# One transfer of 1 MB per unit of streamed weights in place of two transfers of 512 KB

## The chip, the cores and the metric

One core of one Trainium2 chip (trn2) runs the kernel. The metric is the device time of one execution in microseconds (us); lower is better.

## What is computed

One layer of a streaming encoder for 640 tokens (512 of a prompt, 8 x 16 of running streams), all in float32, width 2048. Cut to what matters:

```
p  = x @ w_in                                     # 8448 columns: q, k, v of two mixers, two gates
yA = chunk_band_attention(...); yB = sliding_window_attention(...)
h  = LayerNorm(alpha*x + (sigmoid(gA)*(yA@w_proj_a) + sigmoid(gB)*(yB@w_proj_b)) @ w_out)
y  = LayerNorm(alpha*h + PEER(h))                 # 128*128 experts of one neuron, 8 heads, 16 picks per head

PEER: q = h @ w_query; scores against two sets of 128 keys; top 16 of the 16*16 sums of two top 16s
      act = gelu(u_table[picks] . h); out = sum(gate * act * v_table[picks])
```

## The kernel before

All matrix products go through one stream of weights. `wstream` is a list of units; a unit is 128 partitions x 2048 float32 values, 1 MB, 8 KB in each partition. The program walks through 484 units (`SEGMENTS`, `TOTAL`): 34 of the q, k, v projection for the first 256 tokens, 32 of the gates, 16 each of projection, output and query, the same once more for the other 384 tokens, and then 256 units of the expert tables u and v for the 320 tokens that are computed densely. Each unit is 16 k steps.

A float32 product is made of three products of the reduced type fp32r: the weights are split into a high part (a copy into the reduced type) and a low part (what is left), and so are the moving operands. `k_step`, `act_step` and `part` issue the three matmuls of a k step (high x high, high x low, low x high), so a unit is 48 matmuls. Per unit `n`, with slot `s = n % 2`:

- SP loads the unit into `raw[s]` (`w_raw`), in two halves of 1024 values per partition, `HALVES` (`load`, lines 448 to 451). Each half has a semaphore of its own, `raw_half[s][h]`, and waits until POOL has subtracted the same half of unit `n - 2`: `low_first` counts the first halves, `split_done` the second ones.
- ACT copies each half into `w_hi[s]` (`split_high`, line 969). It waits for the half's landing and for PE to have read the same half of unit `n - 2` (`half_read`, `unit_done`). `split_high(n + 2, 0)` stands in ACT's program ahead of the evacuation of unit `n`, `split_high(n + 2, 1)` behind it.
- POOL subtracts: `w_lo = w_raw - w_hi`, a half at a time (`low`, line 507), when ACT's copy is done.
- PE starts a unit at `low_first` and goes on with its second half at `split_done`.

Every engine takes its instructions in the order of its program. So there are two slots in `w_raw` and two in `w_hi` and `w_lo`, and a half of `w_raw` is free again when POOL has subtracted it.

Beside this stream, 320 tokens get their experts by gathers: `ITEMS` is a list of 649 steps, of which 640 are an indirect DMA of 128 rows of 8 KB (1 MB) from the u or the v table into one of four buffers (`rows`, `fetch`, line 525) and a pass of DVE over them (lines 1483 and 1486). `deal` spreads the steps over the units from `GATHER_AT` on, by the rates in `RATES`, two per unit for most of the last 192. POOL issues the gather of step `r + 4` right behind a `low` of the unit to which step `r` was dealt, after DVE has released its buffer (`rows_used`). DVE takes the steps in order too, between its other work for the units.

The last 192 units are, first, eight groups of 8 u units (activations, line 851) and 8 v units (output, line 906), for which ACT loads 1280 KB of `gate_matrix` each (`load_gates`), and then 64 v units in eight groups whose activations were computed early and are loaded again with the gates (`load_early`: one load of 1280 KB and eight of 160 KB per group).

```
act.wait_ge(raw_half[s][h], 16 * (n // 2) + 16)
if n >= 2:
    act.wait_ge((half_read, unit_done)[h], n - 1)
act.activation(w_hi[s][:, HALVES[h]], raw[s][:, HALVES[h]], ACT.Copy).then_inc(hi_late, 1)
```

Of the kernel before, what the change touches and what calls it, by code (L numbers as in the profile page):

```python
# [54 lines left out]
HALVES = (slice(0, D // 2), slice(D // 2, D))  # L55
# [10 lines left out]
AT = {}  # L66
# [175 lines left out]
def build(nc, x_t, wstream, u_rows, v_rows, cka, cva, ckb, cvb, rext, negs, bp_b, bs_b, sinks, lnp, lnrow, subk, consts, pt_out, y_out, n_out):  # L242
# [3 lines left out]
    ds = bass.ds  # L246

    with ExitStack() as ctx:
# [3 lines left out]
        def sb(name, shape, dt=f32):  # L252
            return ctx.enter_context(nc.sbuf_tensor(name, shape, dt))

        def sem(name):
            return ctx.enter_context(nc.semaphore(name))
# [8 lines left out]
        raw = [sb(f"w_raw{s}", [P, D]) for s in range(2)]  # L265
# [126 lines left out]
            return ap[..., FROM[ph]:FROM[ph] + WIDTH[ph]]  # L392


        raw_half = [[sem(f"raw_half{s}_{h}") for h in range(2)] for s in range(2)]
        hi_late, low_first, split_done, half_read, unit_done = (
            sem(n) for n in ("hi_late", "low_first", "split_done", "half_read", "unit_done"))

# [46 lines left out]

        @block.sync
        def _(sp):
            def load(n, unit, s, h):
                sp.wait_ge((low_first, split_done)[h], n - 1)
                sp.dma_start(raw[s][:, HALVES[h]], wstream[:, ds(unit, 1), HALVES[h]].rearrange("p a c -> p (a c)")) \  # L450
                    .then_inc(raw_half[s][h], 16)

            for s in range(2):
                if s:
                    sp.wait_ge(mv_in[1], 16)
                for h in range(2):
                    sp.dma_start(raw[s][:, HALVES[h]], wstream[:, s, HALVES[h]]).then_inc(raw_half[s][h], 16)

            def table(dst, src):
                sp.dma_start(dst, src).then_inc(tab_done, 16)  # L460

            def bias_table(n):

                rt, n_r = rext.tensor, rext.shape[1]
                if n == 0:
                    table(bp_a[:, 64:P, :], bass.AP(rt, 63, [[n_r, 16], [-1, 64], [1, 512]]))
                elif n == 1:
                    table(bp_a[:, 0:64, 0:448], bass.AP(rt, 127, [[n_r, 16], [-1, 64], [1, 448]]))
                elif n < 6:
                    h = slice(4 * n - 8, 4 * n - 4)  # L470
                    table(bp_a[h, 0:64, 448:512], negs[h])
                elif n < TABLES:
                    b = DEC_T * (n - 6)
                    table(bs_a[:, b:b + DEC_T, :], bass.AP(rt, 383, [[n_r, 16], [-1, 16], [1, 144]]))

            for name, unit, count in SEGMENTS:
                if name == "qkv":
                    for i in range(1, count // 2):
                        for s in range(2):
                            for h in range(2):  # L480
                                load(2 * i + (AT[name] + s), 2 * i + (unit + s), s, h)
                            bias_table(2 * i - 2 + s)
                    continue
                first = 0
                if count == 2:
                    for s in range(2):
                        for h in range(2):
                            load(AT[name] + s, unit + s, s, h)
                    continue
                with sp.Fori(first, count // 2) as i:  # L490
                    for s in range(2):
                        for h in range(2):
                            load(2 * i + (AT[name] + s), 2 * i + (unit + s), s, h)

            for k in range(KT_N):
                sp.wait_ge(ln_out, k + 1)
                sp.dma_start(y_out[k], r_acc[:, k, :]).then_inc(y_out_done, 16)
            sp.wait_ge(y_out_done, 16 * KT_N)
# [458 lines left out]
        def _(act):  # L957
# [3 lines left out]
            def split_high(n, h):  # L961

                s = n % 2
                if n >= TOTAL:
                    return
                act.wait_ge(raw_half[s][h], 16 * (n // 2) + 16)
                if n >= 2:
                    act.wait_ge((half_read, unit_done)[h], n - 1)
                act.activation(w_hi[s][:, HALVES[h]], raw[s][:, HALVES[h]], ACT.Copy).then_inc(hi_late, 1)  # L969
# [4 lines left out]
            def load(dst, src, into):  # L974
                act.dma_start(dst, src).then_inc(into, 16)
# [6 lines left out]
            def qkv_slot(n, i, ph, between=None):  # L982

                s, w = n % 2, WIDTH[ph]
                split_high(n + 2, 0)
                if between is not None:
                    between()
                act.wait_ge(unit_done, n + 1)
                free_ev(s)
                act.activation(ev[s][:, 0:w], acc(s, ph), ACT.Copy, scale=SCALE if i >= ROW_QA else 1.0).then_inc(qkv_evac, 1)  # L990
                split_high(n + 2, 1)
                act.wait_ge(qkv_evac, 2 + N_QKV * ph + i + 1)
                load(cut(pt_out[i], ph), ev[s][:, 0:w], qkv_stored[s])
                stores["qkv"][s] += 1
# [23 lines left out]
            for k in range(KT_N):  # L1018
                if k % 4 == 0:
                    act.wait_ge(mv_in[k // 4], 16)  # L1020
                copy_high(0, k, Rw[0][:, k, :])
                if k % 4 == 3:
                    split_high(k // 8, k // 4 % 2)
# [257 lines left out]
            n = AT["b2"]  # L1281
# [17 lines left out]
            for i in range(B_CHUNKS[4]):  # L1299
                n = AT["b4"] + i  # L1300
# [33 lines left out]
            for m in range(TAIL):  # L1334
                n = AT_EARLY + m
# [11 lines left out]
                if m in (1, 3):  # L1347
                    h = m // 2
# [653 lines left out]
```

## Time and profile before

| | us |
|---|---|
| median of 3 runs | 4365.65 |
| lowest, highest | 4357.78, 4372.58 |
| the profiled execution | 4363.35 |
| its span, first to last instruction | 4361.4 |

The difference of 2 us between the profiled execution and its span lies before the first and behind the last instruction. "Busy" of an engine is the time in which one of its instructions ran; for PE the ends are modelled, and matmuls overlap, so the mean of one is about twice the distance between two. The DMA share is the mean busy share of the core's 16 DMA engines; where packets overlap it can pass 1. In the queues, `q0` holds the DMAs that POOL issues (gathers among them), `q1` those of SP and `q10` those of ACT. PEclk is the granted clock of TensorE as a share of its full 2.4 GHz.

### The profile page before, as it was taken

To read this page: it belongs to the slowest core of one execution; us is meant where nothing else is said; L and a number is where in the kernel's file an instruction comes from. 1 tells how busy PE (TensorE), PEld (TensorE's weight loads), DVE (VectorE), ACT (ScalarE), POOL (GpSimd) and SP (SyncE) were. 2 spreads that over 40 slices of the span, in tenths; PEclk is the share of its full clock that TensorE was granted. 3 is DMA by queue.
4 is the path that set the end of the run, shared out by engine and by line. 5 is a ranking of instruction groups with operands and counts; after the bars stand their busy time and mean duration, and the time that the engine had idled before them with its cause. 6 is when DMAs were issued, how large, how long until landed. Compare 5 with 4: busy or idle time off the path is not lost. (4 is left out here: it accounts for less than half of the span.)

```text
span 4361.4 us, 71495 instructions
## 1 busy us (share of the span) xinstructions
PE 4062.1 (93%) x26789; PEld 3894.4 (89%) x26789; DVE 2803.3 (64%) x4041; ACT 1666.8 (38%) x2837; POOL 2980.6 (68%) x1624
## 2 busy tenths in 40 slices
PE   8999999999999999889799799999999997988997
PEld 8988889999977777889799799999999997988886
DVE  3122222278466688798697677576776766789885
ACT  4433444442233344332333266633333332322333
POOL 7843457675754455678357767688888987888884
PEclk9988999999999999899899899999999999999998
DMA  8755446554998899899246999999999999999993
GB/s 293 225 161 158 132 135 207 163 169 140 375 367 343 335 372 364 336 386 412 93 129 210 389 330 344 332 391 413 417 418 412 413 413 386 412 414 398 414 400 101
DMA packets 366152, 1341.34 MB, mean 308 GB/s; under 512 B 35969, under 2 KB 148481, under 8 KB 280449
## 3 DMA queue, kind: packets, MB, share of 16 engines
q0 software_dynamic: 93760, 682.66, 38.1%
q1 hardware_dynamic: 146992, 515.57, 34.3%
q10 hardware_dynamic: 125200, 140.62, 9.2%
q8 instruction: 105, 1.72, 0.2%
q14 instruction: 95, 0.77, 0.0%
HBM read 1277.73 MB, written 65.80 MB: 308 GB/s over the span
## 5 line engine op out<-in xcount | busy, mean ns | idle before, releaser
L507 POOL TENSOR_TENSOR w_lo<-w_raw,w_hi 128x1024 fp32r<-128x1024 f32 x968 | 2342.3, 2421 | 1129.3 <-ACT w_hi L969 1112.8
L969 ACT ACTIVATE w_hi<-w_raw 128x1024 fp32r<-128x1024 f32 x968 | 1022.1, 1057 | 1469.9 <-DMA w_raw<-in_wstream 869.8
L1486 DVE SCALAR_TENSOR_TENSOR banks<-rows,act_n,banks 128x2048 f32<-128x2048 f32 x320 | 752.6, 2352 | 224.7 <-DMA rows<-in_v_rows,idx_all 221.8
L1483 DVE CUSTOM_DVE_ANT_0 rows<-rows,banks 128x2048 f32<-128x2048 f32 x320 | 728.7, 2282 | 260.7 <-DMA rows<-in_u_rows,idx_all 259.8
L906 PE MATMUL banks<-weighted,w_hi 128*128 128x320 f32 x3072 | 694.3, 315 | 59.4 <-DVE weighted L1853 28.9
L572 PE MATMUL banks<-mv,w_hi 128*128 128x256 f32 x3648 | 693.4, 292 | 18.6 <-POOL w_lo L507 12.7
L572 PE MATMUL banks<-mv_hi,w_hi 128*128 128x384 f32 x1824 | 638.1, 350 | 56.1 <-ACTq L1223 21.5
L851 PE MATMUL banks<-mv_hi,w_hi 128*128 128x320 f32 x2048 | 647.5, 316 | 39.9 <-POOL w_lo L507 36.6
L851 PE MATMUL banks<-mv_lo,w_hi 128*128 128x320 f32 x2048 | 635.6, 310 | 0.0
L851 PE MATMUL banks<-mv_hi,w_lo 128*128 128x320 f32 x2048 | 635.4, 310 | 0.0
L572 PE MATMUL banks<-mv_lo,w_hi 128*128 128x384 f32 x1824 | 620.7, 340 | 0.0
L572 PE MATMUL banks<-mv_hi,w_lo 128*128 128x384 f32 x1824 | 620.2, 340 | 0.0
L572 PEld LDWEIGHTS banks<-mv,w_hi 128*128 128x128 f32 x3648 | 589.0, 199 | 29.3 <-issue 13.4
L906 PEld LDWEIGHTS banks<-weighted,w_hi 128*128 128x128 f32 x3072 | 523.8, 192 | 69.7 <-DVE work L1878 33.1
L572 PE MATMUL banks<-mv,w_lo 128*128 128x256 f32 x1824 | 527.5, 289 | 0.0
L906 PE MATMUL banks<-weighted,w_lo 128*128 128x320 f32 x1536 | 481.2, 313 | 0.0
L572 PEld LDWEIGHTS banks<-mv_hi,w_hi 128*128 128x128 f32 x1824 | 350.7, 192 | 105.8 <-issue 81.4
L851 PEld LDWEIGHTS banks<-mv_hi,w_hi 128*128 128x128 f32 x2048 | 387.6, 189 | 49.7 <-POOL w_lo L507 40.2
L525 POOL DMA_INDIRECT rows<-in_u_rows,idx_all x320 | 321.2, 1004 | 117.9 <-issue 53.3
L851 PEld LDWEIGHTS banks<-mv_lo,w_hi 128*128 128x128 f32 x2048 | 387.8, 189 | 0.0
L851 PEld LDWEIGHTS banks<-mv_hi,w_lo 128*128 128x128 f32 x2048 | 386.9, 189 | 0.0
L525 POOL DMA_INDIRECT rows<-in_v_rows,idx_all x320 | 310.3, 970 | 93.1 <-issue 46.8
(180 smaller groups left out, 5412.1 us busy)
## 6 DMA issues: line engine op xcount, KB each, us to landing
w_raw<-in_wstream SPq DMA_DIRECT2D x968, 512.0 KB, 7.0
gate_matrix<-work ACTq DMA_DIRECT2D x20, 1024.0 KB, 13.9
work<-gate_matrix ACTq DMA_DIRECT2D x16, 1280.0 KB, 10.9
early_act<-work ACTq DMA_DIRECT2D x64, 160.0 KB, 6.3
out_p<-work ACTq DMA_DIRECT2D x34, 192.0 KB, 3.6
gate_scratch<-work ACTq DMA_DIRECT2D x32, 192.0 KB, 7.8
work<-gate_scratch ACTq DMA_DIRECT2D x16, 384.0 KB, 10.2
rows<-in_lnrow POOLq DMA_DIRECT2D x6, 1024.0 KB, 9.3
```

The lines of the kernel that those rows point to most:

```text
L507: pool.tensor_tensor(w_lo[s][:, part], raw[s][:, part], w_hi[s][:, part].bitcast(f32), ALU.subtract) \
L525: pool.indirect_dma_start(rows, None, u_rows if kind == "u" else v_rows, bass.IndirectOffsetOnAxis(ap=idx_at[blk][:, pick:pick + 1], axis= ...
L572: ins = pe.matmul(out, a[s][:, P * k:P * k + P], b[ph][:, k, :], start=(k == first and n == 0), stop=(k == last and n == 2))
L851: last = pe.matmul(banks[:, bank, 0:ND], a[s][:, P * k:P * k + P], b[1][:, k, G3:], start=(k == 0 and n == 0), stop=(k == KT_N - 1 and n = ...
L906: last = pe.matmul(banks[:, dt % 4, 0:ND], a[s][:, at:at + P], b[z][:, e, :], start=(e == 0 and n == 0), stop=(e == EG - 1 and n == 2))
L969: act.activation(w_hi[s][:, HALVES[h]], raw[s][:, HALVES[h]], ACT.Copy).then_inc(hi_late, 1)
L1483: ins = dve.tensor_tensor_reduce(rows, rows, nat, 1.0, 0.0, ALU.mult, ALU.add, weight)
L1486: ins = dve.scalar_tensor_tensor(nat, rows, weight, nat, ALU.mult, ALU.add)
```

## The change

Each unit is loaded by one transfer of 128 x 2048 values, 8 KB per partition, with one semaphore per slot, `raw_in[s]`. SP issues it when both halves of unit `n - 2` are subtracted (`split_done`). Both of ACT's copies wait for this one semaphore. Copies, subtractions and matmuls are made in halves as before.

```diff
--- before.py
+++ after.py
@@ -392,7 +392,7 @@
             return ap[..., FROM[ph]:FROM[ph] + WIDTH[ph]]
 
 
-        raw_half = [[sem(f"raw_half{s}_{h}") for h in range(2)] for s in range(2)]
+        raw_in = [sem(f"raw_in{s}") for s in range(2)]
         hi_late, low_first, split_done, half_read, unit_done = (
             sem(n) for n in ("hi_late", "low_first", "split_done", "half_read", "unit_done"))
 
@@ -445,16 +445,14 @@
 
         @block.sync
         def _(sp):
-            def load(n, unit, s, h):
-                sp.wait_ge((low_first, split_done)[h], n - 1)
-                sp.dma_start(raw[s][:, HALVES[h]], wstream[:, ds(unit, 1), HALVES[h]].rearrange("p a c -> p (a c)")) \
-                    .then_inc(raw_half[s][h], 16)
+            def load(n, unit, s):
+                sp.wait_ge(split_done, n - 1)
+                sp.dma_start(raw[s][:, :], wstream[:, ds(unit, 1), :].rearrange("p a c -> p (a c)")).then_inc(raw_in[s], 16)
 
             for s in range(2):
                 if s:
                     sp.wait_ge(mv_in[1], 16)
-                for h in range(2):
-                    sp.dma_start(raw[s][:, HALVES[h]], wstream[:, s, HALVES[h]]).then_inc(raw_half[s][h], 16)
+                sp.dma_start(raw[s][:, :], wstream[:, s, :]).then_inc(raw_in[s], 16)
 
             def table(dst, src):
                 sp.dma_start(dst, src).then_inc(tab_done, 16)
@@ -477,20 +475,17 @@
                 if name == "qkv":
                     for i in range(1, count // 2):
                         for s in range(2):
-                            for h in range(2):
-                                load(2 * i + (AT[name] + s), 2 * i + (unit + s), s, h)
+                            load(2 * i + (AT[name] + s), 2 * i + (unit + s), s)
                             bias_table(2 * i - 2 + s)
                     continue
                 first = 0
                 if count == 2:
                     for s in range(2):
-                        for h in range(2):
-                            load(AT[name] + s, unit + s, s, h)
+                        load(AT[name] + s, unit + s, s)
                     continue
                 with sp.Fori(first, count // 2) as i:
                     for s in range(2):
-                        for h in range(2):
-                            load(2 * i + (AT[name] + s), 2 * i + (unit + s), s, h)
+                        load(2 * i + (AT[name] + s), 2 * i + (unit + s), s)
 
             for k in range(KT_N):
                 sp.wait_ge(ln_out, k + 1)
@@ -963,7 +958,7 @@
                 s = n % 2
                 if n >= TOTAL:
                     return
-                act.wait_ge(raw_half[s][h], 16 * (n // 2) + 16)
+                act.wait_ge(raw_in[s], 16 * (n // 2) + 16)
                 if n >= 2:
                     act.wait_ge((half_read, unit_done)[h], n - 1)
                 act.activation(w_hi[s][:, HALVES[h]], raw[s][:, HALVES[h]], ACT.Copy).then_inc(hi_late, 1)
```

On SP, the loop over the last units, before:

```order
L490 ISA
L450 ISA [waits low_first]
L450 DMA w_raw<-in_wstream 128x1024
L450 ISA [waits split_done]
L450 DMA w_raw<-in_wstream 128x1024
L449 REGISTER_ALU
L450 ISA [waits low_first]
L450 DMA w_raw<-in_wstream 128x1024
L450 ISA [waits split_done]
L450 DMA w_raw<-in_wstream 128x1024
L490 REGISTER_ALU
```

and now:

```order
L486 ISA
L450 ISA [waits split_done]
L450 DMA w_raw<-in_wstream 128x2048
L449 REGISTER_ALU
L450 ISA [waits split_done]
L450 DMA w_raw<-in_wstream 128x2048
L486 REGISTER_ALU
```

Four issues for two units have become two, each behind the second half's subtraction.

On ACT, at the end of a group of v units and the first u unit of the next (`work<-gate_matrix` is the gates' load, `banks<-banks` the activation of a u unit), before:

```order
L969 ACTIVATE w_hi<-w_raw 128x1024 [waits unit_done,raw_half0_1]
L975 DMA work<-gate_matrix 128x2560 [waits w_prod]
L969 ACTIVATE w_hi<-w_raw 128x1024 [waits half_read,raw_half1_0]
L969 ACTIVATE w_hi<-w_raw 128x1024 [waits unit_done,raw_half1_1]
L969 ACTIVATE w_hi<-w_raw 128x1024 [waits half_read,raw_half0_0]
L969 ACTIVATE w_hi<-w_raw 128x1024 [waits unit_done,raw_half0_1]
```

and now:

```order
L964 ACTIVATE w_hi<-w_raw 128x1024 [waits unit_done,raw_in0]
L970 DMA work<-gate_matrix 128x2560 [waits w_prod]
L964 ACTIVATE w_hi<-w_raw 128x1024 [waits half_read,raw_in1]
L964 ACTIVATE w_hi<-w_raw 128x1024 [waits unit_done,raw_in1]
L964 ACTIVATE w_hi<-w_raw 128x1024 [waits half_read,raw_in0]
L964 ACTIVATE w_hi<-w_raw 128x1024 [waits unit_done,raw_in0]
```

No instruction of ACT has moved. Both copies of a slot now wait for the same semaphore. On PE, DVE and POOL nothing has moved.

## Rows read from the trace of the kernel before

**Rows 1.** The page: busy time and share of each engine.

```profile
PE 4062.1 (93%) x26789; PEld 3894.4 (89%) x26789; DVE 2803.3 (64%) x4041; ACT 1666.8 (38%) x2837; POOL 2980.6 (68%) x1624
```

**Rows 2.** Windows: us, busy (x instructions) per engine, PEclk, DMA share, GB/s.

```profile
593.00:826.00 233.00, 228.90 (x1793) 225.43 (x1791) 52.04 (x124) 102.89 (x141) 173.64 (x72) 0.99 0.64 192
...
2821.00:3309.00 488.00, 466.58 (x3084) 458.14 (x3083) 337.54 (x330) 164.66 (x204) 424.71 (x247) 0.98 1.01 407
3309.00:3807.00 498.00, 462.17 (x3074) 459.15 (x3073) 349.90 (x295) 161.29 (x201) 421.65 (x249) 0.97 1.01 407
3807.00:4254.00 447.00, 404.64 (x2644) 391.89 (x2642) 394.25 (x360) 141.40 (x169) 366.05 (x213) 0.99 1.01 406
```

**Rows 3.** Windows: eight u units, and the border to the v units behind them.

```profile
3549.15:3605.85 56.70, 56.66 (x384) 56.07 (x383) 41.07 (x30) 20.29 (x29) 52.95 (x32) 1.00 1.02 418
3605.85:3618.80 12.95, 8.92 (x50) 8.92 (x51) 8.97 (x9) 4.43 (x7) 10.73 (x7) 0.87 1.02 418
```

**Rows 4.** Waits, 2821 to 4254 us: waiting, released by: us, times, longest.

```profile
ACT w_hi L969 <- DMA w_raw<-in_wstream: 773.7, 308, 6.5
DVE banks L1486 <- DMA rows<-in_v_rows,idx_all: 155.5, 127, 4.3
POOL w_lo L507 <- ACT w_hi L969: 133.5, 179, 8.4
DVE rows L1483 <- DMA rows<-in_u_rows,idx_all: 131.9, 97, 6.7
...
PE banks L906 <- DVE work L1878: 29.9, 29, 3.0
PE banks L906 <- DVE weighted L1853: 28.9, 11, 4.9
PE banks L906 <- POOL w_lo L507: 17.9, 11, 4.6
PE banks L851 <- POOL w_lo L507: 16.3, 4, 14.2
```

**Rows 5.** The chain that ended last, 3840 to 3870 us: start, us, what.

```profile
3851.81 13.16 DMA w_raw<-in_wstream
3864.97 0.02 issue
3864.99 1.07 ACT w_hi L969
3866.06 0.07 issue
3866.13 2.42 POOL w_lo L507
```

**Rows 6.** DMA, 2821 to 4254 us: queues; issues with median us to landing.

```profile
q0 software_dynamic: 49060, 357.23, 60.7%
q1 hardware_dynamic: 52613, 191.54, 33.8%
...
w_raw<-in_wstream SPq DMA_DIRECT2D x365, 512.0 KB, 10.9
work<-gate_matrix ACTq DMA_DIRECT2D x16, 1280.0 KB, 10.9
work<-early_act ACTq DMA_DIRECT2D x32, 160.0 KB, 20.1
x_raw<-early_act ACTq DMA_DIRECT2D x32, 160.0 KB, 28.1
```

**Rows 7.** Timeline of SP and POOL from 3599 us.

```profile
3601.89 0.33 SPq L450 DMA_DIRECT2D w_raw<-in_wstream  x1
...
3599.32 2.41 POOL L507 TENSOR_TENSOR w_lo<-w_raw,w_hi 128x1024 fp32r<-128x1024 f32 x1 [0.25 <-ACT w_hi L969]
3601.88 0.95 POOL L525 DMA_INDIRECT rows<-in_v_rows,idx_all  x1
3603.09 2.41 POOL L507 TENSOR_TENSOR w_lo<-w_raw,w_hi 128x1024 fp32r<-128x1024 f32 x1 [0.26 <-ACT w_hi L969]
```

**Rows 8.** DMA issues: half loads from 700 to 1000 us; a 1 MB store.

```profile
w_raw<-in_wstream SPq DMA_DIRECT2D x87, 512.0 KB, 3.5
...
block_h<-work ACTq DMA_DIRECT2D x1, 1024.0 KB, 3.9
```

**Rows 9.** Timeline of ACT and POOL in the light stretch.

```profile
788.69 1.06 ACT L969 ACTIVATE w_hi<-w_raw 128x1024 fp32r<-128x1024 f32 x1 [1.82 <-PE banks L572]
791.57 1.06 ACT L969 ACTIVATE w_hi<-w_raw 128x1024 fp32r<-128x1024 f32 x1 [1.82 <-PE banks L572]
...
789.83 2.40 POOL L507 TENSOR_TENSOR w_lo<-w_raw,w_hi 128x1024 fp32r<-128x1024 f32 x1 [0.48 <-ACT w_hi L969]
```

**Rows 10.** Timeline of ACT at the start, the copies of unit 1.

```profile
12.95 1.06 ACT L969 ACTIVATE w_hi<-w_raw 128x1024 fp32r<-128x1024 f32 x1 [0.77 <-DMA w_raw<-in_wstream]
...
15.14 1.04 ACT L969 ACTIVATE w_hi<-w_raw 128x1024 fp32r<-128x1024 f32 x1
```

## The prediction

> **What bounds the kernel now.** The page's summary comes first [rows 1]: PE is busy for 93% of the span, the other engines for 38 to 68%. PE is therefore the engine to watch, and a change in the loads can give back only what PE loses while it waits. The table of windows says where that is [rows 2]. From 2821 to 4254 us the DMA engines are busy for a share of 1.01 in all three windows, at 406 to 407 GB/s. One unit is 48 matmuls (16 k steps of three), so 3084, 3074 and 2644 matmuls are 64.3, 64.0 and 55.1 units, and a unit takes 7.60, 7.78 and 8.11 us. Eight units that run without a stall take 56.70 us for 384 matmuls, 7.09 each, with the granted clock at 1.00 [rows 3]; right behind them 12.95 us hold 50 matmuls, a stall of nearly 6 us at the border from u units to v units, while DMA stays at 1.02 and 418 GB/s. These 1433 us lose about 0.7 us per unit, and DMA is full throughout. In the light stretch from 593 to 826 us DMA is busy for 0.64 [rows 2].
>
> The waits of that stretch say who is late [rows 4]: ACT waits 773.7 us for `w_raw`, POOL 133.5 us for ACT, DVE 155.5 + 131.9 us for gathered rows. Seen from PE, 17.9 + 16.3 us go to POOL's `w_lo` and 29.9 + 28.9 us to DVE. The chain shows the loop in one piece [rows 5]: transfer 13.16, copy 1.07, subtraction 2.42, about 0.2 between them, then the next transfer into the same half: 16.9 us for two units, 8.45 each. So a half buffer goes round as fast as its transfer lands, and the transfer is slow since DMA is shared. The queues show how [rows 6]: 365 half loads at 10.9 us each are 2.8 in flight on average over 1433 us, so the weights' queue is never empty. It moved 52613 packets and the gathers' queue 49060. Each row of 128 plus 16 semaphore writes makes 144 per transfer, so these are 365 half loads with rows of 4 KB and 341 gathers with rows of 8 KB. Nearly one row each: the DMA engines take turns by rows, and weights get one third of the bytes that the two share.
>
> **The change part by part.**
>
> *Instructions.* SP loses 484 of 968 issues and their waits. An issue is 0.33 us [rows 7] on an engine that does nothing else: nothing. ACT keeps its 968 copies and POOL its 968 subtractions, at the same places.
>
> *The packets.* Weights' rows become 8 KB. The 4 KB rows cost 33.8% for 191.54 MB, 0.1765% per MB; the gathers' 8 KB rows 60.7% for 357.23 MB, 0.1699% per MB [rows 6]. If weights come to cost what gathers cost, 3.7% of 33.8%, 1.26% of 1433 us, is freed: 18 us. Half as many semaphore writes lie in that figure. The low end is 0, if bytes and not rows are the engines' limit. I take 18, since the gathers are the same engines in the same stretch, and a full resource passes its saving on. Stretches in which PE hides the transfers give nothing for this.
>
> *The turns.* A weight load now takes 8 KB per turn against the gathers' 8 KB. At 418 GB/s [rows 3] a load of 1.05 MB beside gathers needs 2.10 MB of traffic, 5.0 us, where a half of 0.52 MB needs 1.57 MB, 3.8 us, behind 1.8 others. To this comes what a load costs however small. From the light stretch: a half lands in 3.5 us [rows 8], of which 1.25 is data at 418 GB/s, so 2.25. From the full stretch: the 1280 KB load of `gate_matrix`, alone in its queue, lands in 10.9 us [rows 6]; with turns of 10, 8 and 4 KB its 1.31 MB need 2.88 MB of traffic, 6.9 us, so 4.0. A 1 MB load lands in 7.3 to 9.0 us.
>
> *The later start.* The first half's buffer used to be refilled when its own subtraction ended; now it waits for the second. POOL's rows give the gap [rows 7]: subtraction 2.41, gather issue 0.95, subtraction again 3.77 us after the first began. The first half also waits for the whole landing. The loop of a slot becomes: landing, copy 1.07 with 0.1, subtraction 2.4, gather issue and gaps 1.35, subtraction 2.4, 0.15 to the issue, so landing + 7.5. With 7.3 us that is 14.8 for two units, 7.4 each; with 9.0 it is 16.5, 8.25 each. The half loop it replaces gives 8.45 at its worst [rows 5] and 7.69 as the mean of the first 128 units [rows 2]. The bytes alone need 7.4 us there: 1.05 MB of weights, 1.95 of gathers (341 in 183 units) and 0.08 of gates, 3.08 MB at 418 GB/s. So near the low end the loop hides behind the full DMA and costs nothing; that end I take, because a landing above 7.9 us needs gathers in turn all the time, and as soon as DMA is not full there are fewer of them. Ends: 0, and (8.25 − 7.69) × 128 + (8.25 − 8.11) × 55 = +79 us.
>
> *Light stretches.* There a copy starts every 2.88 us on PE's release, and subtractions of 2.40 have 0.48 us between them [rows 9]. A copy at 788.69 is followed by its subtraction from 789.83 to 792.23, and the same half is wanted 11.52 us after the copy, at 800.2. The half used to be there by 792.4 + 3.5 = 795.9. Now the issue is 2.88 us later, at 795.3. A 1 MB landing lies between the 3.9 us of the 1 MB store to `block_h` and 3.5 + 1.25 = 4.75 [rows 8]; I take 4.3, and it is there at 799.6, 0.6 us early. If that cover goes, the next is 5.1 us: a subtraction ends 3.54 us after its copy starts, PE begins that unit 8.64 us after it (the other half of one unit and a whole one, three times 2.88). Cost 0. [...]
>
> *The start.* The first copy of unit 1 waited 0.77 us for its half at 12.95, and the second ran at 15.14 without a wait [rows 10]. Now both wait for the whole: 0 to 2.2 us later, while PE waits for x behind it. I take +1.
>
> *Other queues.* While weights are in turn, ACT's gate load gives up 4 KB more per turn: 8 turns per engine at 26 GB/s, 1.3 us on 10.9. Its wait, and those of the `early_act` loads at 20.1 and 28.1 us [rows 6], are for a group of eight units (some 65 us) ahead. Nothing. For the gathers the same bytes of weights come in fewer, larger bites: on average no later. DVE and then POOL, which issues a gather only when DVE has released its row and is in order with the subtractions, would feel it.
>
> Sum: 4363.35 (the profiled execution) − 18 + 1 = 4346.4; that execution is 2.3 us under the median of 4365.65, so 4349.
>
> **The rivals.**
>
> *Slower: the slot's loop binds.* With one load of 1 MB in flight where 2.8 halves were, the fixed part of each landing is no longer hidden behind the one before. Place: u and v units from 2821 us on. Price: +79 at a landing of 9.0 us, 4445; at 8.3 us the loop is 15.8, 7.9 a unit, +27, 4393. It decides from 7.9 us on (2 × 7.69 − 7.5). For it: the 10.9 us of the gate load. Against it: DMA at 1.01 cannot be slower without becoming idle, and while gathers are in flight it is not. The Trainium skill speaks on this side too (Perfetto Trace Analysis, "DMA Optimizations": splitting lets some data start sooner if DMA engines are generally idle); here they are idle only in the light stretches, where PE covers the loss, so the trace does not make its case. Chance 0.25.
>
> *Nothing.* The packet saving is not real, or PE's stalls at the borders (DVE's and ACT's chain, [rows 3, 4]) set the time: 4366, within 6. For it: 58.8 of PE's 93 us of listed waits are on DVE. Chance 0.27.
>
> *Faster by more.* With half the turns weights are no longer late, and PE's 17.9 + 16.3 us on POOL go too: 4349 − 34 = 4315. Against it: the bytes still need 7.4 us. Chance 0.09.
>
> *The change does not do what it says.* The 8 KB rows are cut into 4 KB or weights keep one third: 1.05 MB then needs 3.15 MB, 7.5 us, a landing of 9.8 to 11.5, a loop of 17.3 to 19.0, at least 8.65 a unit against 7.81 over 183 units: +153, 4519. Against it: the gathers' 144 packets per MB and the 10 KB rows of the gate loads. Chance 0.05.
>
> **How the numbers follow.** The forecast, 4349 with its own range of 4340 to 4352, has 0.34. A change under 0.3%, 13 us, is about what a measurement of this kernel can't tell from none. Faster by more than that: 0.34 + 0.09 = 0.43; within: 0.27; slower: 0.25 + 0.05 = 0.30. The range goes from 4318, most of the third rival, to 4405, beyond the middle of the first; it leaves out the fourth.
>
> **What would show it.** In the profile after: 484 loads of 1024 KB landing in 7 to 8 us from 2821 us on and in about 4 in the light stretch; the weights' queue at 32.5% there for the same bytes; DMA still at 1.0; ACT's 773.7 us on `w_raw` much lower and DVE's 287 us on gathers higher. It is wrong if landings exceed 8 us, if DMA falls under 0.98 with units over 7.8 us, or if PE gets waits on `w_lo` before 1000 us.

## The result and the profile after

The change takes 4470.13 us (median of 4 runs, 4461.43 to 4478.40), the kernel before 4366.41 us (4 runs, 4357.78 to 4372.58): a ratio of 1.0242, 95% interval 1.0226 to 1.0259, some 104 us slower. The forecast was 4349, faster; what happened is the first rival, the slot's loop. The profiled execution took 4461.43 us, its span is 4459.5 us; in it the last unit ends 98.1 us later than in the one before.

The page, busy time and share of each engine ([rows 1] before):

```profile
PE 4089.1 (92%) x26789; PEld 3914.0 (88%) x26789; DVE 2803.1 (63%) x4041; ACT 1646.4 (37%) x2837; POOL 2983.2 (67%) x1624
```

No engine has more to do, so most of the added time is waiting. It is not all: PE's 26789 matmuls are busy for 27.0 us longer, and the mean granted clock of the execution is 0.961, before 0.966; the other 71.1 of the 98.1 us are idle time of PE. The windows come next, cut at the same units as [rows 2] (columns: us, busy (x instructions) of PE, PEld, DVE, ACT, POOL, PEclk, DMA share, GB/s):

```profile
605.00:838.00 233.00, 228.90 (x1794) 225.60 (x1793) 54.24 (x124) 103.22 (x144) 173.72 (x72) 0.99 0.57 190
2849.00:3371.00 522.00, 473.64 (x3083) 462.80 (x3082) 338.92 (x331) 157.43 (x199) 424.11 (x247) 0.97 0.97 381
3371.00:3897.00 526.00, 470.97 (x3074) 462.39 (x3072) 345.28 (x296) 157.59 (x202) 423.45 (x250) 0.96 0.98 388
3897.00:4351.00 454.00, 405.51 (x2597) 395.49 (x2598) 396.66 (x358) 132.07 (x165) 360.72 (x210) 0.96 0.99 393
```

In the light stretch PE's busy time is the same to the hundredth (its DMA share fell from 0.64 to 0.57 for nearly the same bytes; see the packets below). In the two windows of 64 units, 488 and 498 us became 522 and 526: 8.13 and 8.22 us per unit. DMA, at 1.01 and 407 GB/s before, is now at 0.97 to 0.99 and 381 to 393. A full resource became one with gaps. Units 292 to 483 as a whole, before and then now:

```profile
2821.66:4332.56 1510.90, 1401.76 (x9224) 1377.14 (x9224) 1118.75 (x1034) 484.88 (x593) 1255.13 (x724) 0.98 0.97 391
```

```profile
2849.23:4430.61 1581.38, 1423.43 (x9224) 1393.19 (x9223) 1120.68 (x1034) 467.18 (x587) 1254.58 (x724) 0.97 0.95 374
```

Of the 70.5 us between them PE is idle for 48.8, and its 9224 matmuls take 21.7 more at the lower granted clock. How much of these 21.7 the waits would have hidden, no run shows.

Waits of the same stretch, 2849 to 4351 us ([rows 4] before: waiting, released by, us, times, longest):

```profile
ACT w_hi L964 <- DMA w_raw<-in_wstream: 923.6, 172, 14.2
POOL w_lo L502 <- ACT w_hi L964: 213.5, 114, 10.6
DVE banks L1481 <- DMA rows<-in_v_rows,idx_all: 171.7, 96, 5.7
DVE rows L1478 <- DMA rows<-in_u_rows,idx_all: 147.8, 71, 6.7
...
PE banks L846 <- POOL w_lo L502: 47.1, 31, 11.1
PE banks L901 <- POOL w_lo L502: 43.2, 25, 7.6
```

PE's wait for POOL's `w_lo` was 34.2 us and is 90.3. POOL waits for ACT for 213.5 in place of 133.5, ACT for the transfer for 923.6 in place of 773.7, and in 172 waits in place of 308: nearly once for each of the 182 loads, 5.4 us each. The queues and loads of that stretch ([rows 6] before):

```profile
q0 software_dynamic: 49036, 357.03, 59.5%
q1 hardware_dynamic: 26225, 190.99, 32.7%
...
w_raw<-in_wstream SPq DMA_DIRECT2D x182, 1024.0 KB, 8.9
work<-gate_matrix ACTq DMA_DIRECT2D x16, 1280.0 KB, 11.8
```

26225 packets are 144 for each of 182 loads, so rows are 8 KB, and the load lands in a median of 8.9 us: the change does what it says. One loop of one slot, from the timeline (start us, us, engine, line, operation; in brackets the idle time before and what ended it), in the order in which things follow one another:

```profile
3099.82 0.33 SPq L450 DMA_DIRECT2D w_raw<-in_wstream  x1
3109.71 2.01 ACT L964 ACTIVATE w_hi<-w_raw 128x1024 fp32r<-128x1024 f32 x2 [5.69 <-DMA w_raw<-in_wstream]
3110.85 2.40 POOL L502 TENSOR_TENSOR w_lo<-w_raw,w_hi 128x1024 fp32r<-128x1024 f32 x1 [1.80 <-ACT w_hi L964]
3113.41 0.95 POOL L520 DMA_INDIRECT rows<-in_u_rows,idx_all  x1 [0.15 <-issue]
3114.38 2.41 POOL L502 TENSOR_TENSOR w_lo<-w_raw,w_hi 128x1024 fp32r<-128x1024 f32 x1
3116.96 0.33 SPq L450 DMA_DIRECT2D w_raw<-in_wstream  x1
```

17.14 us from one issue to the next into the same slot, 8.57 per unit. ACT waited 5.69 us and then made both copies at once ("x2", 2.01 us), since the whole unit had landed at once; for 9.89 us nothing worked for this slot but the transfer, and for the 7.25 us behind that no transfer ran for it. On average 182 × 8.9 / 1502 = 1.08 loads are in flight, where it was 2.8 halves.

**Stage by stage.** The times at which units end are the events of `unit_done` in the traces. "Two halves" and "one load" say how the stage is loaded.

| stage (units) | before, us | the change | e9: one load from unit 292 on | e10: one load until unit 291 | spread of other runs with two halves there |
|---|---|---|---|---|---|
| qkv (0 to 33) | 218.5 | +6.3 | +0.7, two halves | +7.0 | +0.7 |
| gate, attention 1 (34 to 65) | 374.9 | +6.0 | +8.9, two halves | +6.5 | −2.8 to +9.4 |
| 66 to 147 | 614.8 | +0.6 | −0.1 | +1.7 | −0.7 (e12 alone) |
| gate 2 (148 to 179) | 537.7 | +6.4 | +0.7 | +1.4 | −8.2 to +0.6 |
| proj 2 (180 to 195) | 176.1 | +8.1 | +3.4 | +8.8 | −0.7 to −0.3 |
| 196 to 291 | 899.8 | +0.1 | +3.5 | +3.3 | +0.2 to +1.8 |
| 292 to 419 | 985.8 | +61.9 | +65.8 | −0.3, two halves | −1.9 to +6.8 |
| 420 to 483 | 525.1 | +8.5 | +14.2 | −0.2, two halves | −5.9 to −2.2 |

The last column is e11 and e12 below; e12 has an edit of its own in units 292 to 419, where its +6.8 is. What is the change's: 61.9 + 8.5 in the full stretch; some 7 in proj 2 (PE is idle there for 27.1 us, 27.5 in e10, and for 19.8 to 22.0 in the kernels with two halves; e9's +3.4 is partly slower matmuls); and 6 or 7 in qkv, 1.0 of it at the start, where unit 0 ends at 27.6 in place of 26.6 us.

The gate stages differ by some 12 us between executions of the same loads. In the first one the granted clock accounts for it. Its windows in the kernel before, in the change, in e9 and in e12 (only the second has one load):

```profile
218.48:593.34 374.86, 359.82 (x2742) 326.54 (x2741) 97.26 (x369) 155.00 (x395) 153.52 (x65) 0.92 0.48 145
```

```profile
224.77:605.67 380.90, 363.92 (x2742) 330.25 (x2741) 97.36 (x369) 154.94 (x395) 155.21 (x66) 0.91 0.44 144
```

```profile
219.14:602.89 383.75, 367.27 (x2742) 333.03 (x2741) 94.88 (x369) 155.50 (x395) 153.41 (x65) 0.90 0.47 142
```

```profile
219.22:591.31 372.09, 356.77 (x2742) 323.93 (x2741) 97.77 (x369) 154.78 (x395) 153.58 (x65) 0.93 0.49 146
```

The matmuls are the same 2742; their busy time goes from 356.8 to 367.3 us as the clock goes from 0.93 to 0.90, and PE's idle time stays at 15.0 to 17.0 us. So 4.1 of the change's 6.0 us there are clock, and it is not the loads that make the stage vary. In gate 2 the change's 6.4 us are idle time of PE (50.5 us for 44.0; 43.2 to 45.6 in e9, e11 and e12, 47.1 in e10): some of it is probably the change's.

### The profile page after: what moved, and what is told of

The parts are those of the page before. It is cut to its first block and busy times, and to the rows that moved or that the text cites. A ratio compares the mean times of both kernels' runs of the same rounds, so it can differ in the third digit from the quotient of the medians.

```text
span 4459.5 us, 70123 instructions
## 1 busy us (share of the span) xinstructions
PE 4089.1 (92%) x26789; PEld 3914.0 (88%) x26789; DVE 2803.1 (63%) x4041; ACT 1646.4 (37%) x2837; POOL 2983.2 (67%) x1624
## 5 line engine op out<-in xcount | busy, mean ns | idle before, releaser
L901 PEld LDWEIGHTS banks<-weighted,w_hi 128*128 128x128 f32 x3072 | 525.1, 193 | 93.7 <-DVE work L1873 49.0
L567 PEld LDWEIGHTS banks<-mv,w_lo 128*128 128x128 f32 x1824 | 364.4, 200 | 0.0
```

The source lines that it names most:

```text
L567: ins = pe.matmul(out, a[s][:, P * k:P * k + P], b[ph][:, k, :], start=(k == first and n == 0), stop=(k == last and n == 2))
L901: last = pe.matmul(banks[:, dt % 4, 0:ND], a[s][:, at:at + P], b[z][:, e, :], start=(e == 0 and n == 0), stop=(e == EG - 1 and n == 2))
```

## The experiments

Kernels measured together shared their runs of the kernel before, whose medians were 4368.31 (e1 to e4), 4365.01 (e5 to e8), 4366.14 (e9 to e12), 4363.18 (e13) and 4367.41 (e14).

### e1, e2, e3: the two waits that one transfer makes, with two transfers kept

The change brings two waits: the first half's load is issued later (when both subtractions are done), and the first copy waits for the whole unit. Each was put alone into the kernel before, then both.

```diff
 # e1_late_issue
-                sp.wait_ge((low_first, split_done)[h], n - 1)
+                sp.wait_ge(split_done, n - 1)
 # e2_whole_wait
-                act.wait_ge(raw_half[s][h], 16 * (n // 2) + 16)
+                act.wait_ge(raw_half[s][0], 16 * (n // 2) + 16)
+                act.wait_ge(raw_half[s][1], 16 * (n // 2) + 16)
 # e3_both_4k: both edits
```

> The kernel before with one part of the change: two transfers of 512 KB with a semaphore each, but both issued only when the second half of unit n - 2 is subtracted. Theory A (the loop of a slot binds: landing, copy, two subtractions with a gather issue between, next issue): the first half of this transfer still lands first and its copy and subtraction overlap the second's landing, so most of the lost lead is hidden; between 4370 and 4410 us. Theory B (rows of 8 KB in the weights' queue disturb the gathers and lower the DMA rate from 407 to about 388 GB/s): rows here are 4 KB, so within 10 us of before, and the DMA rate from 2850 us on back at 407 GB/s.

> The kernel before with the other part of the change: halves are issued at their own subtractions as before, but both of ACT's copies wait until both halves of the unit have landed. Theory A: the first half's subtraction comes later, its slot is freed later; slower than before by 30 to 120 us, with the weights landing in 8 to 10 us from 2850 us on. Theory B: within 10 us of before.

> Both parts together, still as two transfers of 512 KB with rows of 4 KB: the waits of the change without its rows and its single transfer. Theory A: at least as slow as the change (4470 us), up to 4600 us, since weights get a third of the shared bytes and not half, so that the second half lands in 9 to 11 us. Theory B: under 4400 us, for the rows of 8 KB are gone.

Measured: e1 4414.28 us, ratio 1.0105 (1.0087 to 1.0123); e2 4398.88, 1.0073 (1.0055 to 1.0091); e3 4587.77, 1.0492 (1.0465 to 1.0520). e1 lies 4 us above the top of what Theory A gave. Over their median before each wait costs, 46 and 31 us, and both together cost 219, far over their sum. In the profiled executions units 292 to 483 alone took 27, 29 and 168 us more. With one wait a half is still in flight while the other is worked on; with both nothing of that slot is. So the larger rows are not what hurts. On the contrary, with the same waits the change is 118 us faster than e3 (109 by the ratios).

### e4: both subtractions in a row, gathers behind them

To shorten the loop by the gather's issue, POOL does both subtractions of a unit first.

```diff
-                for h, part in enumerate((STEPS[n][:first], STEPS[n][first:])):
+                for h, part in enumerate(((), STEPS[n])):
```

> The change with one edit on POOL: both subtractions of a unit back to back, the unit's gathers behind the second. Theory A: the gather issue of 0.95 us with its gap of 0.15 leaves the slot's loop, so 1.1 us per two units or 0.55 per unit over 183 units, up to 100 us back: 4370 to 4420 us. Theory B: the rows are the same, 4460 to 4480 us, or slower since gathers are issued later.

Measured: 4703.59 us, 1.0780 (1.0761 to 1.0799). A miss by over 280 us. 202 us of its loss lie in gate 2 (740.2 us for 537.7), where `RATES` gives a unit 4.2 gathers on average, which now come in one bunch, and 59 in units 420 to 483, where the change has 8.5. In units 292 to 419 it took 1028.4 us where the change took 1047.7.

### e5, e6: less to move

Both leave out part of the computation and so free DMA time: the v passes fetch half of each row and work on old values for the rest. e5 keeps the two halves, e6 has the change.

```diff
-                    pool.indirect_dma_start(rows, None, u_rows if kind == "u" else v_rows,
+                    table = u_rows if kind == "u" else v_rows
+                    if kind == "v":
+                        rows, table = rows[:, 0:D // 2], table.rearrange("e (a c) -> (e a) c", a=2)
+                    pool.indirect_dma_start(rows, None, table,
```

> The kernel before with less traffic: the gathers of the v passes (320 of 640) fetch 128 rows of 4 KB in place of 8 KB; the second half of the columns of those passes works on old rows, so that part of the experts' output is left out. Everything else, DVE's passes too, is as before. It is the partner of the next run. Theory A (the slot's loop, in which the landing is the part that grows with the other traffic): in the 32 units from 356 to 387, whose steps are all v, the 239.8 us of before fall to 230 to 235 (7.1 to 7.3 per unit, PE's own 7.04 and the borders), since DMA is no longer full.

> The change with the same cut in traffic. Theory A: in units 356 to 387 the landing of a load falls from 7.7 to 5 or 6 us, the loop to under 2 x 7.1 us, and the difference to the kernel before, 12.5 us in these units, falls under 4 us, while in units 292 to 323, whose steps are all u with full rows, it stays at 14 to 22 us. Theory C (what costs is not the loop but the later release of POOL and ACT, at fixed cost per unit, with traffic or without): the difference stays at 10 us or more in both.

Measured: e5 4284.26 us (2 runs), e6 4380.39 (5 runs): 96 us apart, so the change costs nearly as much with less to move. Units 356 to 387 in the windows, e5 and then e6:

```profile
3281.20:3506.40 225.20, 225.20 (x1537) 225.20 (x1536) 168.87 (x125) 78.89 (x96) 214.34 (x126) 1.00 0.88 305
```

```profile
3330.30:3567.00 236.70, 228.88 (x1539) 225.34 (x1538) 164.76 (x125) 76.20 (x96) 211.77 (x125) 1.00 0.83 286
```

With two halves PE never stops (225.20 of 225.20) and DMA has room. With one load it loses 11.4 us in 32 units at a DMA share of only 0.83. The waits say why, e6 and then e5:

```profile
ACT w_hi L967 <- DMA w_raw<-in_wstream: 146.7, 32, 10.4
```

```profile
ACT w_hi L972 <- PE banks L909: 68.5, 27, 5.2
```

In e5 ACT waits for PE, so the weights are there first. In e6 it waits for the load in each of the 32 units. The expectation missed all the same: Theory A had a difference under 4 us here, and it is 11.4, where Theory C's number (10 or more) came true. e5 itself came out under its 230 to 235 us. For e6 Theory A had the landing fall to 5 or 6 us and the loop to under 14.2; the landing fell to 6.5 (mean 6.56) and the loop to 14.85. What speaks for the loop and against a fixed cost per unit is that every one of the 32 first copies starts within 0.35 us of its landing, and that the 70 units of e11 below cost nothing. In units 292 to 323, with full rows, the difference is 17.0 us, as expected. The argument of the prediction, that a loop cannot bind once DMA has gaps, falls here.

### e7, e8: the loop from inside

e7 is e4's order for units 292 to 419 only, e8 has ACT do its gelu ahead of the first copy in u units.

```diff
 # e7_one_pool_uv
-                for h, part in enumerate((STEPS[n][:first], STEPS[n][first:])):
+                for h, part in enumerate(((), STEPS[n]) if AT_LATE <= n < AT_LAST else (STEPS[n][:first], STEPS[n][first:])):
 # e8_gelu_first
-                split_high(n + 2, 0)
...
+                split_high(n + 2, 0)
```

> The change with both subtractions of a unit back to back and its gathers behind them, but only for units 292 to 419, where at most two gathers belong to a unit. Run e4 did this everywhere and lost 202 us in the attention of the second part, where four gathers belong to a unit, while it won 19 us against the change in these 128 units. Theory A: 4445 to 4455 us, 15 to 25 us under the change; the gain is less than the 1.1 us per loop since gathers then start later. If it is 4470 or more, the gather issue between the subtractions is no part of what binds.

> The change with one edit on ACT: in the u units the activation of unit n (gelu) stands ahead of the first copy of unit n + 2, so that ACT, when the load is late, does not hold back the activation. Theory A as the slot's loop alone: no change, 4465 to 4478 us. Theory D (ACT, blocked on the whole load in its program's order, holds back gelu, DVE's product and so PE): 4430 to 4455 us.

Measured: e7 4456.99 us, 1.0211 (1.0187 to 1.0235), 13 below the change; e8 4470.04, 1.0242 (1.0223 to 1.0261), no difference. That ACT, blocked on a late load, holds back the gelu behind it is not where the time goes. e7 is 2 us above what was expected at most. In its profiled execution e7 is only 3 us shorter than the change in the units whose order it alters, so where its 13 us lie is not shown, and its interval overlaps the change's.

### e9, e10, e11: the one load in one part only

```diff
+def whole(n):
+    return n >= AT_LATE
...
-                act.wait_ge(raw_half[s][h], 16 * (n // 2) + 16)
+                act.wait_ge(raw_in[s] if whole(n) else raw_half[s][h], 16 * loads_before(n) + 16)
```

SP issues one load for a unit where `whole(n)` holds, and the two halves elsewhere; `loads_before(n)` counts the earlier loads of the same kind into the slot. This is e9; e10 has `n < AT_LATE`, e11 `AT["b0"] <= n < AT["b4"] + 12`, units 66 to 135.

> The kernel before up to unit 291; from unit 292 on (the u and v units of the stretch in which DMA is full) each unit is loaded by one transfer of 1 MB with one semaphore, as in the change. Theory A (the cost is local: each stage pays by itself for the whole landing that ACT waits for): units 292 to 483 cost what they cost in the change, 18.3 + 15.9 + 12.5 + 15.3 + 8.5 = 70.5 us, so 4366 + 70 = 4437, between 4430 and 4445, and the stages before unit 292 stand as before within 2 us. Theory B (the late stages pay for what the early ones push into them, gathers that are behind when unit 292 begins): less than 50 us over before, under 4416.

> The other part alone: one transfer of 1 MB for units 0 to 291, two halves from unit 292 on. Theory A: 6.3 + 6.0 + 0.1 + 0.5 + 6.4 + 8.1 - 1.2 + 1.4 = 27.6 us, so about 4394, between 4386 and 4402, and the sum of both parts is the change's 104 within 8 us. Theory B: over 45 us, above 4411, since the late stages start with a backlog. My prediction of the change had these stages at 1 us.

> One transfer of 1 MB only for units 66 to 135, where PE sets the pace and DMA is busy for 0.6; two halves everywhere else. Theory A: no difference, within 4 us of before (0.1 us in these stages in the change), because the next landing of 4.9 us is there before the same half is wanted again. Theory B (484 fewer issues and semaphore writes were worth something there): faster by more than 4 us. If it is slower by more than 8 us, the transition between the two ways costs, or PE does wait.

Measured: e9 4460.58 us, 1.0203 (1.0168 to 1.0238), by the ratio +89; e10 4396.58, 1.0074 (1.0049 to 1.0099), +32; e11 4366.14, 1.0003 (0.9989 to 1.0017). Windows of 292 to 419 and 420 to 483, e9 and then e10:

```profile
2838.80:3890.40 1051.60, 947.51 (x6153) 926.52 (x6152) 684.58 (x626) 315.33 (x401) 847.90 (x496) 0.97 0.97 383
3890.40:4429.60 539.20, 478.07 (x3072) 467.80 (x3072) 435.05 (x409) 152.31 (x187) 407.45 (x229) 0.96 0.89 348
```

```profile
2850.50:3836.00 985.50, 930.27 (x6152) 918.46 (x6150) 688.90 (x624) 323.66 (x399) 845.42 (x496) 0.97 1.01 408
3836.00:4360.90 524.90, 473.97 (x3072) 461.42 (x3072) 430.73 (x412) 158.51 (x188) 408.58 (x229) 0.97 0.91 360
```

In e10 the late units run as before, DMA back at 1.01 and 408 GB/s, although they start later; no backlog is handed on. In e9 they cost 80 us (65.8 + 14.2), more than the 50 that the backlog theory allowed and 10 more than in the change. So the full stretch pays where it has the one load. That the parts add up is only roughly shown: by the ratios they make 121 against the change's 106, where 8 us of difference were expected at most; the intervals reach 15 and 11 us to each side. e9's total lies 16 us above what was expected of it at most (4445), and its stages before unit 292 are not within 2 us of before but 17 over in its profiled execution: 8.9 in the first gate stage, most of it clock, 3.4 in proj 2 and 3.5 in units 196 to 291. And e11 puts one load on the 70 units in which PE covers it: nothing, one way or the other. That 70 of 140 issues are gone there is worth nothing that can be measured.

qkv was to be free by the prediction. ACT's waits from 0 to 226 us, e10 (one load) and e9 (two halves):

```profile
ACT w_hi L994 <- DMA w_raw<-in_wstream: 94.5, 32, 6.1
ACT work L1015 <- PE banks L597: 17.3, 9, 7.3
```

```profile
ACT work L1015 <- PE banks L597: 58.7, 31, 8.0
ACT w_hi L994 <- PE banks L597: 39.0, 28, 1.8
ACT w_hi L994 <- issue: 11.0, 2, 8.3
ACT w_hi L994 <- DMA w_raw<-in_wstream: 8.0, 4, 3.6
```

With two halves ACT waits for PE, with one load it waits for the load, 32 times in the 34 units. Most of that is slack that PE does not see; 6 to 7 us come through, in idle time of PE (21.3 us in e10, 18.3 in e9) and in slower matmuls.

### e12: e7's order on the kernel before

> The kernel before (two halves) with one edit: in units 292 to 419 POOL issues a unit's gathers behind both subtractions in place of between them. It is the control for the same edit on the change, which gave 13 us back. Theory A (there the gather's issue stood in the slot's loop, which is as long as landing + the work behind it): with two halves the first half's loop has no gather issue in it and only the second half comes round 0.95 us earlier, so less than the change got, 0 to 10 us faster. Theory B (the order helps by itself, whatever the loads): 10 us or more faster, about 4353.

Measured: 4372.98 us, 1.0023 (1.0010 to 1.0036): a little slower, which neither theory had. In the loop of the two halves the gather's issue between the subtractions costs nothing. No version here that computes everything beats the kernel before.

### e13, e14: the number of transfers or the size of the rows

e3 and the change have the same waits, and differ in rows (4 and 8 KB) and in transfers (two and one). These two have rows of 8 KB in two transfers of 512 KB, cut by partitions, and the change's waits; e13 as in the diff, e14 with `(slice(0, P, 2), slice(1, P, 2))`.

```diff
-                sp.dma_start(raw[s][:, :], wstream[:, ds(unit, 1), :].rearrange("p a c -> p (a c)")).then_inc(raw_in[s], 16)
+                for p in (slice(0, 64), slice(64, P)):
+                    sp.dma_start(raw[s][p, :], wstream[p, ds(unit, 1), :].rearrange("p a c -> p (a c)")).then_inc(raw_in[s], 16)
...
-                act.wait_ge(raw_in[s], 16 * (n // 2) + 16)
+                act.wait_ge(raw_in[s], 32 * (n // 2) + 32)
```

> The change with the 1 MB of a unit in two transfers again, but cut by partitions (64 each) and not by columns: rows stay 8 KB, both are issued together when both subtractions are done, and ACT waits for both. So waits are those of the change and of e3_both_4k, rows those of the change, the number of transfers that of e3_both_4k. Theory A (the 118 us between e3_both_4k and the change come from the rows' size, turns by rows): like the change, 4470, between 4455 and 4485, landing of both 9 us in the full stretch. Theory B (they come from the second transfer and its semaphore writes, or from the issue of 0.33 us ahead of it): near 4588, above 4530.

> As e13_two_by_rows, with the two transfers cut into even and odd partitions in place of the lower and the upper 64. Rows are 8 KB as in the change, transfers two as in e3_both_4k, waits those of both. e13_two_by_rows took 5468 us, since 512 KB into 64 adjoining partitions kept the DMA engines busy for 39.2% of 5471 us for 515.57 MB, 4.2 engine-us per MB where the change's loads took 2.6; so it said nothing of its question. Theory A (the 118 us between e3_both_4k and the change come from the rows' size): 4470, between 4455 and 4490. Theory B (from the second transfer): near 4588, above 4530. Theory C on e13_two_by_rows (64 partitions in one transfer are the trouble, adjoining or not): again over 4800, and then rows against transfers stays open.

Measured: e13 5468.37 us, 1.2532 (1.2511 to 1.2553); e14 4558.16, 1.0438 (1.0404 to 1.0472). e13 says nothing of the question, and is told below. e14, with the change's rows, is 88 us over the change and 30 under e3 (86 and 24 by the ratios): most of the 118 us belong to the second transfer, some 30 at most to the size of the rows (e14 also has the spread-out partitions). Theory A had it the other way. 3000 to 4300 us in e3, e14 and the change, in this order:

```profile
3000.00:4300.00 1300.00, 1117.02 (x7129) 1092.57 (x7128) 872.51 (x791) 357.52 (x455) 986.73 (x581) 0.95 0.96 366
```

```profile
3000.00:4300.00 1300.00, 1133.55 (x7240) 1105.89 (x7238) 876.78 (x801) 364.89 (x464) 999.69 (x588) 0.95 0.97 372
```

```profile
3000.00:4300.00 1300.00, 1170.06 (x7586) 1144.35 (x7585) 939.86 (x848) 382.31 (x486) 1051.12 (x617) 0.97 0.99 392
```

Four kernels issue at the end of both subtractions. Means over units 292 to 419 from the traces' events, us from the issue:

| kernel | first copy done | first subtraction | second subtraction | (that + 0.16) / 2 | unit measured |
|---|---|---|---|---|---|
| e1, first copy needs its half only | 8.62 | 11.77 | 15.70 | 7.93 | 7.88 |
| the change | 9.70 | 12.63 | 16.29 | 8.23 | 8.19 |
| e14, 8 KB rows, two transfers | 10.63 | 13.41 | 17.06 | 8.61 | 8.57 |
| e3, 4 KB rows, two transfers | 10.67 | 13.56 | 17.21 | 8.69 | 8.65 |

A unit is half a loop, as it must be with two slots whatever binds (before: 15.54 / 2 = 7.77 against 7.70 measured), so that the last two columns agree is no proof. What shows that the change's loop binds is that it has no slack: in 121 of the 128 units the first copy starts within 0.35 us of the landing, the work goes on from there, and the next issue comes 0.16 us behind the second subtraction. From the first copy on, all four have 6.4 to 7.1 us; what differs is the time until the copy, 1 us more for two transfers that are both waited for than for one.

## Why the prediction was wrong

- **The later start.** This step failed. It had the loop as landing + 7.5 and took the low end, cost 0, "because a landing above 7.9 us needs gathers in turn all the time, and as soon as DMA is not full there are fewer of them". The landing was 8.9 us (median; mean 8.35 in units 292 to 419), near the upper bound of 9.0, the loop 16.45 (16.29 + 0.16), 8.2 per unit, where DMA gives a unit in 7.4 by the prediction's own sum. DMA did stop being full (0.97 to 0.99), and the landing stayed above 7.9. e6 has a DMA share of 0.83, and its loop binds all the same. The other end of the bracket was right: +79 by its sum, 70.4 in the profiled execution, 80 in e9. The mean of a unit was 8.19 in units 292 to 419, where I had 8.25.
- **The mechanism behind it.** A full DMA was a sign that enough loads were in flight, not a reserve. With 2.8 halves in flight the copies and subtractions of one load lay beside the transfer of the next. With one load per slot, transfer and work take turns, and DMA has gaps that nobody fills. e1, e2 and e3 show it: 46, 31, and 219 us for both.
- **The turns.** Taken 7.3 us, bounds 7.3 to 9.0: inside, at the wrong end. The light stretch: taken 4.3, bounds 3.9 to 4.75; 45 loads from 700 to 1000 us landed in a median of 4.9, outside. The cover still held, with PE's busy time in the window unchanged at 228.90, and e11 confirms it. Nearly all of the cover was used up: in units 66 to 135 the first copy came 5.1 us (median) behind the landing, and now comes 0.7 behind it, in 30 of the 70 units within 0.35 us. The picture behind the sum, turns by rows, is not borne out: by it a load in rows of 4 KB moves in 7.5 us and one in rows of 8 KB in 5.0, but in e3 (4 KB) and e14 (8 KB) the first copy is done 10.67 and 10.63 us after the issue.
- **The work behind the landing.** Taken 7.5. Measured 16.29 − 9.70 = 6.6 from the end of the first copy, 1.06 for the copy, 0.16 to the issue: 7.8. Nearly right; the other 8.6 of the loop is the time until the first copy begins.
- **The packets.** 18 us were taken off, none came. Per MB of weights each of the 16 DMA engines was busy for 2.53 us (33.8% of 1433 us for 191.54 MB) and is for 2.57 (32.7% of 1502 us for 190.99 MB). In the full stretch the low end, bytes and not rows, was right. In the light stretch there is a saving, and it is hardly the rows either. From 700 to 1000 us the kernel before has 51.6% for 46.14 MB, 3.36 us per MB; the change and e1, whose two halves have 4 KB rows and are issued together, have

```profile
q1 hardware_dynamic: 6500, 47.35, 46.5%
```

```profile
q1 hardware_dynamic: 12960, 47.19, 47.3%
```

which is 2.95 and 3.01. PE covers it all there.
- **Light stretches and other queues, "Nothing".** Right for the covered units (66 to 147: +0.6; e11). Wrong for qkv (+6.3, in e10 +7.0) and proj 2 (+8.1, in e10 +8.8, of which the spread may be 3), which I never looked at: I costed one light stretch and let it stand for all 292 units ahead of the full one. In qkv waits end on loads: ACT's 10.0 us in 5 waits for `w_raw` up to 250 us became 99.7 in 32. In proj 2 they do not: ACT never waits for `w_raw` there, the first copy comes 3.9 us (median) behind the landing, and what grew is PE's wait for DVE (18.1 us for 8.4) and ACT's for `gate_scratch` (64.8 for 56.9). The later issue alone, e1, has +9.4 there, the whole wait alone, e2, +0.2; how the later issue gets to PE is not shown.
- **The start**, +1: unit 0 ends 1.0 later.
- **The rival.** "It decides from 7.9 us on" was true. At 8.3 us it gave +27, at 9.0 +79; it missed the 11 to 15 us of qkv and proj 2, and the chance of 0.25 was too low. Of what I held against it, "DMA at 1.01 cannot be slower without becoming idle" was no argument: it became idle. The Trainium skill's sentence (Perfetto Trace Analysis, "DMA Optimizations"), that splitting may help where DMA engines are generally idle, I had set aside since they were not idle here. The measurement says that splitting also matters with DMA full, if it keeps transfers in flight during the work on the data.

Of the 98.1 us between the two profiled executions, 71.1 are idle time of PE and 27.0 slower matmuls, 21.7 of these in the full stretch; the prediction had no term for the clock.

Open: why the landing is 8.9 us and not 7.3, when DMA is only 0.98 busy; why e7's order helps the change by 13 us if it does; how the later issue costs proj 2 some 7 us; and how much of gate 2's 6.4 us is the change's. No run tried a third slot, which by the loop should hide the landing again.

## What to carry to other kernels

Before merging two loads, write down the loop of one buffer: issue, landing, work until the buffer is free, next issue. Divide by the number of buffers; if that is near the pace of the consumer or above it, the halves are what hides the landing, and a DMA share near 1 is their effect and no cover. Where the consumer is clearly slower (the 70 units here: 4.9 + 7.5 = 12.4 us, 6.2 a unit by estimate, against PE's 7.3), one or two transfers made no difference.

## What the runs showed of the hardware

Loads cut by adjoining partitions are slow and slow the gathers beside them. Loads of 512 KB from 700 to 1000 us, e13 (64 adjoining partitions), then e14 (every other partition):

```profile
q1 hardware_dynamic: 6605, 43.28, 64.3%
```

```profile
q1 hardware_dynamic: 7200, 47.19, 46.1%
```

Per MB each DMA engine is busy for 4.46 against 2.93 us, with the same rows and sizes; e13's halves land in 6.1 us where those of the kernel before take 3.5 [rows 8]. In the full stretch of e13, gathers of unchanged form come to 3.35 us per MB (56.9% of 1200 us for 203.91 MB from 3700 to 4900 us), against 2.44 before [rows 6]: they pay too. The Trainium skill (DMA: Bandwidth & Descriptors, "Rules for kernel authors") says of two transfers to disjoint halves of the partitions only that they serialize and are not worth it, and asks for 128 partitions in one. The trace agrees with the advice, and shows its price: 25% more time than the kernel before. Every other partition cost 4.4% in all, e14's longer loop included. What in the chip is shared between adjoining partitions, no run here shows.
